# Moving the later modulation sums of a DeltaNet projection from VectorE to GpSimd

## The reference, cut to what matters

```python
def adaln(c, w, b, n):
    m = jax.nn.silu(c) @ w + b
    return [t[:, None, :] for t in jnp.split(m, n, axis=-1)]
...
shift, scale, gate = adaln(c, a_mod_w[j], a_mod_b[j], 3)
h = rms_norm(x, a_pre_g[j]) * (1 + scale) + shift
y = gated_deltanet(h, a_w_in[j], a_conv_w[j], a_a_log[j], a_dt_bias[j], a_o_gain[j], a_w_out[j])
x = x + gate * rms_norm(y, a_post_g[j])
...
# inside gated_deltanet
proj = h @ w_in
qkv = causal_dwconv_silu(qkv, conv_w)      # 4 taps over time, then SiLU
q = l2_norm(q.reshape(bsz, seq, A_HEADS, A_DK))
k = l2_norm(k.reshape(bsz, seq, A_HEADS, A_DK))
```

## Time and profile before

| | |
|---|---|
| median of 3 runs | 3166.53 us (3164.77 to 3168.99) |
| the profiled execution | 3164.77 us, its span 3163.1 us |
| busy: PE, PEld | 3028.8 us (96%), 2287.5 us (72%) |
| busy: DVE, ACT, POOL | 1740.6 us (55%), 1233.3 us (39%), 726.8 us (23%) |
| mean granted TensorE clock | 0.985 |

### The profile page before, as it was taken

How to read it: one execution, slowest core, us unless ns; L and a number is a source line. 1 busy time by engine, 2 the same in 40 slices (tenths; PEclk the granted TensorE clock), 3 DMA queues, 4 the chain that set the end, 5 groups by cost and what they waited for, 6 DMA issues and landing times.

```text
span 3163.1 us, 39933 instructions
## 1 busy us (share of the span) xinstructions
PE 3028.8 (96%) x15148; PEld 2287.5 (72%) x15148; DVE 1740.6 (55%) x2759; ACT 1233.3 (39%) x2161; POOL 726.8 (23%) x596
## 2 busy tenths in 40 slices
PE   6999999999968997999999999999999999999998
PEld 5777777888857887888878888886555555555687
DVE  5666654657645666555313221104877877778543
ACT  5455556444414555334222212210444444445411
POOL 0000000232225553000000000001555555555300
PEclk9999999999988999999999999999999999999999
DMA  6344423767645665557534421126254442331343
GB/s 228 108 140 140 140 75 97 223 210 208 194 122 204 231 222 159 159 178 226 147 107 97 125 88 73 74 74 160 71 141 107 105 106 76 91 94 51 94 144 122
DMA packets 291083, 428.04 MB, mean 135 GB/s; under 512 B 74654, under 2 KB 187942, under 8 KB 285756
## 3 DMA queue, kind: packets, MB, share of 16 engines
q1 hardware_dynamic: 261612, 359.19, 38.2%
q0 software_dynamic: 13168, 50.42, 5.1%
q10 hardware_dynamic: 16112, 15.86, 1.7%
HBM read 274.58 MB, written 150.69 MB: 134 GB/s over the span
## 4 chain that ended last, share of the span: by engine, by line
PE 56%; DVE 1%; ACTq 1%; issue 1%; ACT 1%; POOL 0%; DVEq 0%; POOLq 0%
PE at_ps L1874 8%; PE at_ps L1925 6%; PE at_ps L1777 6%; PE at_ps L1912 6%; PE at_ps L1779 6%; PE at_ps L1778 5%; PE at_ps L1856 5%; PE at_ps L1859 4%; PE at_ps L1842 3%; PE at_ps L1790 2%; PE at_ps L1791 2%; PE at_ps L1792 2%; ACTq L2377 1%; PE at_ps L1888 1%; ACT at_probs L2474 1%
## 5 line engine op out<-in xcount | busy, mean ns | idle before, releaser
L2474 ACT ACTIVATE at_probs<-at_ps 128x512 f32<-128x512 f32 (+3 forms) x640 | 331.8, 534 | 337.6 <-PE at_ps L1859 272.7
L2098 DVE TENSOR_REDUCE at_partial<-at_ps 128x1 f32<-128x512 f32 (+3 forms) x640 | 370.8, 605 | 140.9 <-PE at_ps L1842 108.7
L106 PE MATMUL pa_y<-pa_h_high,pa_w_high 128*128 128x512 f32 x992 | 395.4, 399 | 4.8 <-ACT pa_ybuf L813 4.8
L108 PE MATMUL pa_y<-pa_h_high,pa_w_low 128*128 128x512 f32 x992 | 387.1, 390 | 0.0
L107 PE MATMUL pa_y<-pa_h_low,pa_w_high 128*128 128x512 f32 x992 | 386.7, 390 | 0.0
L1554 POOL TENSOR_TENSOR at_plain<-at_plain,at_probs 128x512 f32<-128x512 f32 (+3 forms) x256 | 310.2, 1212 | 224.4 <-ACT at_probs L2474 208.7
L1777 PE MATMUL at_ps<-at_h_high,at_w_high 128*128 128x512 f32 x768 | 299.6, 390 | 1.0 <-DVE at_w_low L2027 0.9
L1779 PE MATMUL at_ps<-at_h_high,at_w_low 128*128 128x512 f32 x768 | 298.8, 389 | 0.0
L1778 PE MATMUL at_ps<-at_h_low,at_w_high 128*128 128x512 f32 x768 | 298.8, 389 | 0.0
L1856 PE MATMUL at_ps<-at_h_low,at_h_high 67*128 67x512 f32 (+3 forms) x640 | 260.3, 407 | 11.8 <-ACT at_probs L2474 11.6
L1859 PE MATMUL at_ps<-at_h_low,at_h_high 128*128 128x512 f32 (+3 forms) x640 | 252.7, 395 | 0.0
(11 more groups left out here) (344 smaller groups left out, 5216.6 us busy)
## 6 DMA issues: line engine op xcount, KB each, us to landing
at_h_low<-s_Q SPq DMA_DIRECT2D x96, 256.0 KB, 6.8
s_qkv<-pa_sil POOLq DMA_DIRECT2D x16, 1024.0 KB, 6.6
pa_sil<-s_qkv SPq DMA_DIRECT2D x16, 1024.0 KB, 6.6
dr_kv<-s_qkv SPq DMA_DIRECT2D x16, 1024.0 KB, 8.6
s_Q<-at_parts SPq DMA_DIRECT2D x64, 256.0 KB, 4.1
at_h_high<-s_K SPq DMA_DIRECT2D x32, 512.0 KB, 5.5
pa_wraw<-in_a_w_in_dram ACTq DMA_DIRECT2D x15, 1024.0 KB, 8.8
pa_gb<-in_b_mod_w_dram SPq DMA_DIRECT2D x16, 512.0 KB, 4.5
```

What stands on the lines that cost most here:

```text
L106: nc.tensor.matmul(out, w_high[:, k], h_high[:, k], start=k == 0, stop=False)
L108: ins = nc.tensor.matmul(out, w_low[:, k], h_high[:, k], start=False, stop=k == KC - 1)
L2098: reduced.done(v.tensor_reduce(partial[:, u % 2, h * NQ + sub, grp:grp + 1], rough[:, j % 3, 0:width], AX.X, ALU.max))
L2474: probs_ok.done(a.activation(probs[:, R % 2, t, h, off:BLK], logits[:, l % 3, off:BLK], ACT.Exp))
```

## The change

The six later pieces are summed on GpSimd in place of VectorE. `begin_mod` and VectorE's `later_mod` go; GpSimd has a `later_mod(T)` ahead of its wait for `scaled` of tile T. A step is now two instructions: the weight block is multiplied in place by the column of `csil` (TENSOR_SCALAR, L407 of the new program), and added into `macc` (TENSOR_TENSOR, L411), with a semaphore wait after each. The ring of weight buffers has two places in place of three (the two `gb` tiles; `X` is no longer used for it), so a load waits for the step before the last one.

```diff
-        junk, mw, macc, mrow = flat_tile(Bd), (xs[2], xs[3], xs[5]), xs[4], flat_tile(Bd)[0:1]
+        junk, mw, macc, mrow = flat_tile(Bd), (xs[2], xs[3]), xs[4], flat_tile(Bd)[0:1]
...
             for m in range(KC * len(later)):
-                if m >= len(mw):
-                    sp.wait_ge(mod_step, m - len(mw) + 1)
+                if m >= 2:
+                    sp.wait_ge(mod_step, m - 1)
                 load_mod(m)
                 if m % KC == 1 and m > KC:
                     store_mod(m // KC - 1)
...
-            def begin_mod(piece):
-
-                if piece == 0:
-                    pool.wait_ge(turned_x, NB * KC)
-                else:
-                    pool.wait_ge(mod_summed, piece)
-                g.memset(macc, 0.0).then_inc(mod_zero, 1)
-                pool.wait_ge(mod_zero, piece + 1)
-                w, b, j = later[piece]
-                pool.dma_start(macc[0:1], b[j * D:(j + 1) * D].unsqueeze(0)).then_inc(mb_in, 16)
+            def later_mod(T):
+
+                piece = T // 2
+                if T % 2 == 0:
+                    if T == 0:
+                        pool.wait_ge(turned_x, NB * KC)
+                        pool.wait_ge(c_ready, 1)
+                    else:
+                        pool.wait_ge(mod_summed, piece)
+                    g.memset(macc, 0.0).then_inc(mod_zero, 1)
+                    pool.wait_ge(mod_zero, piece + 1)
+                    w, b, j = later[piece]
+                    pool.dma_start(macc[0:1], b[j * D:(j + 1) * D].unsqueeze(0)).then_inc(mb_in, 16)
+                    pool.wait_ge(mb_in, 16 * (piece + 1))
+                for k in range(T % 2 * KC // 2, (T % 2 + 1) * KC // 2):
+                    m = piece * KC + k
+                    pool.wait_ge(mw_in[m % 2], 16 * (m // 2 + 1))
+                    g.tensor_scalar(mw[m % 2], mw[m % 2], csil[:, k:k + 1], None, ALU.mult).then_inc(mod_term, 1)
+                    pool.wait_ge(mod_term, m + 1)
+                    if m:
+                        pool.wait_ge(mod_step, m)
+                    g.tensor_tensor(macc, macc, mw[m % 2], ALU.add).then_inc(mod_step, 1)
 
             for T in range(QK):
-                if T % 2 == 0 and T // 2 < len(later):
-                    begin_mod(T // 2)
+                if T < 2 * len(later):
+                    later_mod(T)
                 scaled.wait(pool, T)
                 pool.dma_start(s_qkv[:, :, T].rearrange("c p j -> p c j"), chunk_major(sil[:, :])).then_inc(stored, 16)
...
-            def later_mod(T):
-
-                if T == 0:
-                    dve.wait_ge(c_ready, 1)
-                if T % 2 == 0:
-                    dve.wait_ge(mb_in, 16 * (T // 2 + 1))
-                for m in range(T * KC // 2, (T + 1) * KC // 2):
-                    dve.wait_ge(mw_in[m % len(mw)], 16 * (m // len(mw) + 1))
-                    if m:
-                        dve.wait_ge(mod_step, m)
-                    v.scalar_tensor_tensor(macc, mw[m % len(mw)], csil[:, m % KC:m % KC + 1], macc, ALU.mult, ALU.add).then_inc(mod_step, 1)
...
-                        if T < 2 * len(later):
-                            later_mod(T)
```

More of the change, by code:

```diff
@@ L222, in deltanet_projection @@
             "squared_x", "logged_x", "rooted_x", "scaled_x", "turned_x", "h_scaled", "h_rounded", "h_made"))
-        mw_in = [st.sem(f"mw_in{s}") for s in range(len(mw))]
+        mw_in = [st.sem(f"mw_in{s}") for s in range(2)]
         mb_in, mod_step, mod_summed, mod_copied, mod_stored = (st.sem(n) for n in (
             "mb_in", "mod_step", "mod_summed", "mod_copied", "mod_stored"))
-        mod_zero, summed_mod = (st.sem(n) for n in ("mod_zero", "summed_mod"))
+        mod_zero, mod_term, summed_mod = (st.sem(n) for n in ("mod_zero", "mod_term", "summed_mod"))
         block = st.block()
@@ L247, in load_mod @@
                 w, b, j = later[m // KC]
-                sp.dma_start(mw[m % len(mw)], w[m % KC * P:(m % KC + 1) * P, j * D:(j + 1) * D]).then_inc(mw_in[m % len(mw)], 16)
+                sp.dma_start(mw[m % 2], w[m % KC * P:(m % KC + 1) * P, j * D:(j + 1) * D]).then_inc(mw_in[m % 2], 16)
             def store_mod(p):
```

## The result

The changed kernel is slower: 3215.02 us (median of 4 runs, 3204.41 to 3220.05) against 3167.76 in the runs beside it. The ratio is 1.015, its 95% interval 1.0128 to 1.0173: 47 us. The profiled execution took 3207.62 us (span 3205.9), that of before 3164.77 (3163.1). So the direction and the cause at L521 were as forecast, and the time lies in the range, but the loss is two and a half times the 19.0 us of the sum.

What follows compares the result with a forecast made beforehand. TensorE was taken to bound the kernel; its stalls of 1.6 (tile 0), 1.1 (tile 1), 2.7 (tile 3) and 13.6 us (tiles 5, 7, 9, 11) made 19.0, so 3185.5 us against 3166.53, range 3168 to 3220.

Steps and rivals of the forecast that it cites:

- the cause at L521: TensorE's sum of the former tile's squares, its tightest wait: 1.70 us to spare for tile 3, then it stands.
- the sum: Stalls of TensorE over tiles 0, 1, 3, 5, 7, 9, 11: 19.0 us in all; chance 0.50, range 3176 to 3192.
- Turn-taking: VectorE and GpSimd operations run in turn: VectorE held 0.9 us by a multiply, 2.0 by an add.
- the prediction's rule: An operation of GpSimd keeps VectorE back for about its length less 0.37 us.
- held chain: Tile 3's scaling and convolution on VectorE end 4.4 us late; less 1.70 of cover, TensorE stands for 2.7 us.
- Removing VectorE's steps: 48 multiply-adds, 61.6 us of VectorE, stand behind the convolution and TensorE does not wait for them; gain 0.
- What is added on GpSimd: 48 multiplies (1.27 us taken, bounds 956 ns and 2364 ns) and 48 adds (2364 ns); four steps 15.5 us a tile.
- Tile 3: Hand trace of steps 8 to 11: store of tile 2 goes 1.5 us late, still ready before the convolution; stall 2.7.
- rival B: TensorE's clock: stalls of 2.7 to 3.4 us halve it, tiles 3 to 11 lose 8.5 more, 3194; chance 0.14.
- A: Rival: GpSimd as the bound, step of 5.0 us, TensorE waiting at L514; 3212; chance 0.18, including anything between.
- C: Rival: not slower, pending GpSimd operations passed over, convolution keeps its 8.4 us; 3166.5; chance 0.15 with what comes near.
- D: Rival: faster, which would take a wait of TensorE on VectorE's moved steps; chance 0.03.

Runs made afterwards that it cites:

- e7: Changed kernel with the multiply in four forms by piece (constant, column broadcast as second input, plain copy, column as before); 3214.2 us, one run.
- e1: Changed kernel with each step's multiply replaced by a one-input select of the same shape; 3191.4 us, ratio 1.0073 to before.
- e10: e5 with the store of the scaled tile issued from ScalarE's queue; 3185.7 us, ratio 1.0059 to before.
- e2: Changed kernel with the multiply of each step left out, the adds kept; 3214.9 us, ratio 1.0149 to before.
- e5: Kernel before with only the even tiles' steps (24 of 48) moved to GpSimd, ring of three buffers; 3213.8 us, ratio 1.0142.
- e4: Changed kernel with each step replaced by five memsets of 0.95 us, the sums left out; 3171.1 us, ratio 1.0003 to before.
- e3: Changed kernel with the store of the scaled tile issued from ScalarE's queue in place of GpSimd's; 3218.2 us, ratio 1.0140 to before.
- e9: Changed kernel with two accumulators in turn, so a piece need not wait for the sum of the former one; 3211.6 us, ratio 1.0131 to before.
- e12: e9 with memset and bias load of the next piece moved ahead of the odd tile's store; 3226.4 us, ratio 1.0175 to before.
- e11: Kernel before with the gates' two exponentials and two logarithms on ScalarE grouped by table; 3172.8 us, ratio 1.0006 to before.

## Why the prediction was right in sign and short by more than half

**Held by the numbers.** TensorE waits for squares, and those of even tiles (from 2 on) cost at most 0.4. Turn-taking: a pending add holds VectorE by 2.0 us (forecast 2.0), a multiply by 0.7 to 0.9 (0.9). For the multiply that is luck: by the prediction's rule, the instruction's length less 0.37, one of 2.85 us would hold VectorE by 2.5. The rule holds for the add (2.0), the select and the copy of 1.03 (0.66) and the broadcast product of 1.88 (1.5), and fails for the multiply. The convolution of tile 3 ends in time for a stall of 2.3 from the held chain alone (forecast 2.7). Over all tiles, the stalls less the time that SiLU began after the convolution are 30.0 - 14.4 = 15.6, where the sum had 19.0 (tiles 0 and 1 took 3.9 for 2.7, the five odd tiles from 3 on 11.1 for 16.3). Removing VectorE's steps brought nothing, and the weights' landings (median 3.6 us) were no limit.

**The step that failed is "What is added on GpSimd".** It took 1.27 us for the multiply and 2.364 as its upper bound; the kernel shows

```profile
L407 POOL TENSOR_SCALAR pa_gb<-pa_gb,pa_csil x48: 2834/3285/5433, 99.9 to 460.8; 128x1024 f32<-128x1024 f32 x48
L411 POOL TENSOR_TENSOR pa_PT<-pa_PT,pa_gb x48: 2343/2410/4497, 102.8 to 464.5; 128x1024 f32<-128x1024 f32 x48
```

2.83 at its fastest, dearer than the two-input add. So the value taken was less than half of the real one and the upper bound was none; the memset held as a lower bound but said little. All three came from rows of other instructions. The Trainium skill's figure for such a body (GPSIMD Engine Reference, section "3.1 Elementwise"), 0.88 us by the estimate in the prediction, is off by a factor of three for this multiply; the copy of e7, 1.03, is near it. From this one price follows the next step of the prediction, "Tile 3": four steps of 15.5 us became 25.4, so the store of tile 2 did not go 1.5 us late and hidden, but 6.6 us after the scaling, and SiLU began 3.0 us after the convolution. The store would have stayed hidden up to about 25.4 - 3.0 = 22.4 us of steps; with the multiply at 1.27 they would have had about 19 (25.4 - 4 x 1.58). Both are estimates from the rows above; e1, whose store is on time, bears them out. In tiles 3 to 11 this is 3.0 + 3.0 + 2.5 + 3.0 + 2.9 = 14.4 us of stalls.

**The clock, a term that "The sum" put at nothing, failed too.** The sum had 0, rival B 8.5 for stalls of 2.7 to 3.4; the kernel lost 12.7, behind the first stall of 2.3 and the five of 4.6 to 5.5. In e1, with stalls of 1.4 to 3.4, only two of seven brought a dip, in e10 one of six; in e2, with one of 2.29 and six of 5.05, all did.

So 15.6 (held chain, forecast 19.0), 14.4 (store, forecast 0) and 12.7 (clock, forecast 0) make 42.7, nearly the 42.8 of span; the 1.5 ahead of the stage and the 2.4 unexplained are about what later stages give back. e1 puts a cheap instruction in its place, and 18.7 of stalls and clock are left; e10 takes the late store from e5 and most of the clock's loss goes with it; e4 keeps the length of an undisturbed step and takes nearly all turn-taking away, and all of it goes.

**The rivals.** A had nearly the right price (a step of 5.0; it is 5.25) and nearly the right time (3212), but the wait it named, at L514, is not in the changed kernel; it is in e3, once the store no longer binds first. That its 60 us for two tiles came out is no proof of its cause: e5 has the same pace with GpSimd half idle. Two tiles take 60.4 us in the changed kernel ((454.02 - 212.54) / 4, from the squares of tile 3 to those of tile 11). B was right in kind. C is excluded by the held multiply-adds, D by the result.

**Shown and not shown.** Shown by a pair of runs: what the dear multiply does (after, e1), the late store (e5, e10), that a full GpSimd is free where VectorE hardly takes turns with it (e4), that TensorE would wait for GpSimd's piece next (e3). The price of the multiply is read from all 48 of them and again from e7's one run. Argued only: the exact split between store and held chain in the changed kernel, which reads off SiLU's start. Not shown: the loop that e9 and e12 looked for. Not explained: why the multiply of 2.85 us holds VectorE by so little, e2's first multiply-add, e12's sum, and 2.4 us of the changed kernel.

## What to carry to other kernels

Take the price of an instruction from a row of that very instruction on that engine; if there is none, a row of another instruction is no upper bound (here the multiply took 2.83 us and the two-input add 2.34), and the range must say so. When work moves to another engine, look at what stands behind it in that engine's queue (here a store whose landing frees the tile) and work out how long the work may be before that becomes late. Work that VectorE has to take turns with is free only in VectorE's gaps: half of it can cost as much as all (e2, e5), and moving it earlier can cost more (e12), depending on which instruction it meets.

## What the hardware showed that was not expected

- On GpSimd, 128x1024 in float32: multiply by a column 2.83 us, by a constant 2.76, by a column broadcast as second input 1.88, add 2.34, copy 1.03, select 1.03, memset 0.95.
- How long an instruction of GpSimd holds VectorE is not its length: the multiply of 2.85 us holds it by 0.7 to 0.9, the multiply by a constant (2.76), the copy and the select (1.03) all hold a multiply-add by 0.66, the broadcast product of 1.88 by 1.5, the add of 2.35 by 2.0. A memset holds scaling and multiply-adds by nothing, but the first tap, with its one input, by up to 0.7.
- The granted clock fell to half around every stall of 4.6 us and more, and around some of the shorter ones, the shortest 1.79 (e12), 1.98 (e11) and 2.00 (e1); a stall of 2.36 in e1 brought none. The length of the stall alone does not decide.
